# Both directions of a recurrence level in one operation, a pair's gates evacuated raw, and another order of the first block's projections

## The reference

```
f = lb + (1 - lb) * sigmoid(z);  logf = log(max(f, F_TINY));  k = (1 - lb) * sigmoid(-z)
o[t] = sum over s <= t of (q[t] * k[s] * exp(b[t] - b[s])) v[s]      # b = cumsum(logf), q = silu(q_rec)
o_r = o_forward + o_backward; o_r *= rsqrt(mean(o_r * o_r) + EPS); rec = o_r * rec_norm_w * silu(g_rec)
```

## Time and profile before

| | us |
|---|---|
| median of 3 runs | 3002.67 (3001.07 to 3006.88) |
| the profiled execution | 2999.89 |
| its span, first to last instruction | 2998.1 |
| PE / DVE / ACT / POOL busy | 2800.7 / 1654.3 / 1118.8 / 612.9 |
| layer 0 of the first block, first projection matmul to the first of `w_out` | 66.3 to 399.5 |
| layer 1 of the same | 849.8 to 1167.2 |
| last projection matmul of the two | 324.2, 1088.5 |

### The profile page before, as it was taken

How to read it: one execution, slowest core, us unless ns; L and a number is a source line. 1 busy time by engine, 2 the same in 40 slices (tenths; PEclk the granted TensorE clock), 3 DMA queues, 4 the chain that set the end, 5 groups by cost and what they waited for, 6 DMA issues and landing times.

```text
span 2998.1 us, 36465 instructions
## 1 busy us (share of the span) xinstructions
PE 2800.7 (93%) x14716; PEld 2157.6 (72%) x14716; DVE 1654.3 (55%) x3003; ACT 1118.8 (37%) x1875; POOL 612.9 (20%) x338
## 2 busy tenths in 40 slices
PE   3999889999999988999998999989998999999998
PEld 2966667778877766788886878656676878766676
DVE  6767945654464785665456467634425237734424
ACT  3254344322234344443223552243313462343312
POOL 0000024776700000455540231000110131000110
PEclk7999799999999979999999999989999999999999
DMA  7442123544521211344433332111222212121222
GB/s 229 146 125 60 52 85 112 169 140 155 176 83 55 64 55 57 109 140 144 140 127 102 114 113 92 59 61 43 78 77 91 82 43 71 57 85 43 72 72 82
DMA packets 301463, 289.24 MB, mean 96 GB/s; under 512 B 7152, under 2 KB 298096, under 8 KB 301296
## 3 DMA queue, kind: packets, MB, share of 16 engines
q1 hardware_dynamic: 299008, 278.84, 29.2%
q0 software_dynamic: 960, 5.51, 0.5%
q10 hardware_dynamic: 1328, 2.57, 0.3%
HBM read 284.80 MB, written 2.10 MB: 96 GB/s over the span
## 4 chain that ended last, share of the span: by engine, by line
PE 83%; DVE 9%; ACT 4%; POOL 2%; DMA 2%; issue 1%; DVEq 0%; ACTq 0%; POOLq 0%
PE ps L503 81%; PE ps L672 2%; DVE ca L1244 1%; DVE wl L1238 1%; DVE adaacc L1244 1%; DVE recat L1452 1%; POOL raw L1698 1%; DVE hl L1244 1%; POOL raw L1701 1%; ACT wh L836 1%; DMA raw<-in_w_up 1%; DMA xT<-in_xT 0%; ACT rr L836 0%; DVE rawt L1244 0%; DVE s L1491 0%
## 5 line engine op out<-in xcount | busy, mean ns | idle before, releaser
L503 PE MATMUL ps<-hh,wh 128*128 128x512 f32 x2288 | 940.9, 411 | 50.6 <-DVE hl L1244 23.0
L503 PE MATMUL ps<-hh,wl 128*128 128x512 f32 x2288 | 902.4, 394 | 0.0
L503 PE MATMUL ps<-hl,wh 128*128 128x512 f32 x2288 | 902.0, 394 | 0.0
L1238 DVE TENSOR_TENSOR wl<-raw,wh 128x2048 fp32r<-128x2048 f32 (+2 forms) x186 | 443.2, 2383 | 372.3 <-ACT wh L836 371.9
L503 PEld LDWEIGHTS ps<-hh,wh 128*128 128x128 f32 x2288 | 434.9, 190 | 194.0 <-issue 67.9
L503 PEld LDWEIGHTS ps<-hh,wl 128*128 128x128 f32 x2288 | 434.8, 190 | 96.4
L503 PEld LDWEIGHTS ps<-hl,wh 128*128 128x128 f32 x2288 | 436.2, 191 | 89.4 <-issue 7.0
L836 ACT ACTIVATE wh<-raw 128x2048 fp32r<-128x2048 f32 (+2 forms) x186 | 342.6, 1842 | 236.1 <-PE ps L503 142.7
L1698 POOL TENSOR_TENSOR raw<-raw,cond 128x2048 f32<-128x2048 f32 x40 | 186.6, 4664 | 272.5 <-DMA raw<-in_w_ada 272.5
L836 ACT ACTIVATE rawt<-ps 128x512 f32<-128x512 f32 (+1 forms) x106 | 63.3, 597 | 350.4 <-PE ps L503 350.3
L1701 POOL TENSOR_TENSOR raw<-raw 128x1024 f32<-128x1024 f32 x80 | 167.9, 2099 | 6.3
(11 more groups left out here) (229 smaller groups left out, 3772.7 us busy)
## 6 DMA issues: line engine op xcount, KB each, us to landing
raw<-in_w_in SPq DMA_DIRECT2D x74, 1024.0 KB, 5.3
raw<-in_w_ada SPq DMA_DIRECT2D x64, 1024.0 KB, 5.3
raw<-in_w_up SPq DMA_DIRECT2D x44, 1024.0 KB, 5.3
raw<-in_w_in SPq DMA_DIRECT2D x44, 512.0 KB, 5.2
raw<-in_w_out SPq DMA_DIRECT2D x16, 1024.0 KB, 5.2
raw<-in_w_down SPq DMA_DIRECT2D x16, 1024.0 KB, 5.4
stage<-in_w_ada SPq DMA_DIRECT2D x8, 1024.0 KB, 12.3
raw<-in_w_down SPq DMA_DIRECT2D x8, 768.0 KB, 4.6
```

Source lines behind the costliest of these rows:

```text
L503: return e.matmul(o, a, b, start=start, stop=stop, skip_group_check=True)
L1238: return e.tensor_tensor(o, a, b, op)
```

## The change

- Levels: one `rl` unit does both directions. PE makes the same matmuls, into one pair of banks for both directions, even levels into banks 4 and 5 and odd ones into 2 and 3. DVE's queries, keys, totals and conditional copies span both directions in one operation each (`both`).
- The query after silu is kept once, in `M.sg[:, p, :]`; the diagonal's matmuls read it there for both directions, and DVE makes both directions of `recq` in one product, beside the diagonal instead of after it.
- `z` is evacuated raw into `recf`; a new unit `zs` (`gates`) takes both sigmoids later. So the z tiles of pair p wait for level 0 of pair p - 1 instead of level 8. The output and norm of pair p - 1 (`ra`, `ro`, `rn`) are woven around the diagonal of pair p; the square lies in `M.tots[0]`.
- Projections come in the order of `BLOCK1`; `g` tiles are held by `rn` 0, `rn` 1 and `rd` 2.
- `weave` takes, of the side lists that are due, the one with most remaining work; a list whose next unit is an attention score or exponent counts double. `COST` has new figures. This rule holds for the second block too.

The core of the diff (longer removed runs are left out, as they stand above):

```diff
-    "z": (("ACT", 1.25, True),), "q": (("ACT", 0.6, True), ("DVE", 0.7, True), ("ACT", 1.2, True), ("DVE", 2.8, True)),
+    "z": (("ACT", 0.6, True),), "q": (("ACT", 0.6, True), ("DVE", 0.7, True)), "zs": (("ACT", 2.2, True), ("DVE", 2.5, True)),
+    "ra": (("ACT", 2.4, True),),
-    "a": (("ACT", 0.6, True), ("DVE", 0.9, True)), "rd": (("PE", 1.8, True), ("ACT", 1.2, False), ("DVE", 1.4, True)),
-    "rl": (("PE", 1.0, True), ("DVE", 2.1, True)), "ro": (("PE", 2.0, True), ("ACT", 0.6, True)),
+    "a": (("ACT", 0.6, True), ("DVE", 0.9, True)), "rd": (("DVE", 1.2, True), ("PE", 1.8, True), ("ACT", 1.2, False)),
+    "rl": (("PE", 1.6, True), ("DVE", 1.4, True), ("DVE", 1.6, False)), "ro": (("PE", 2.0, True), ("ACT", 0.6, True)),
     "rn": (("PE", 0.9, True), ("ACT", 1.3, True), ("DVE", 1.5, True)), "cv": (("DVE", 3.1, True),),
...
+WEIGHT = {"s1": 2.0, "sx": 2.0}
...
-            first = min(open_, default=None)
+            due = [(sum(left[i]) * WEIGHT.get(sides[i][0][0][0], 1.0), when, i) for when, i in open_ if when <= self.clock["PE"] + 0.2]
+            first = max(due)[1:] if due else None
             main = parts or mains and all(x in done for x in mains[0][3] or ())
-            if first is not None and (first[0] <= self.clock["PE"] + 0.2 or not main):
-                when, i = first
+            if first is not None or not main:
+                when, i = first or min(open_)
                 unit = sides[i].pop(0)[0]
+                left[i].pop(0)
                 done[unit] = ready[i] = self.run(unit, when)
...
+def both(a, first, apart, dims):
+    return bass.AP(a.tensor, a.offset + first, [list(a.ap[0]), [apart, 2]] + dims)
...
     def rec_diagonal(l, p):
-        go.wait_ge(*at("q_in", l, p))
-        go.wait_ge(*at("gates", l, p))
+        go.wait_ge(*at("q_silu", l, p))
+        go.wait_ge(*at("keys", l, p))
         banks_ = [rec_bank(2 + h, ("rd", l, p, h)) for h in range(2)]
         for i in range(NT):
             for d in range(2):
                 for h in range(2):
                     r, sl = rows_of(h), slice(512 * d + 128 * i, 512 * d + 128 * i + 128)
-                    m = mm(banks_[h][:, 128 * i:128 * i + 128], M.reck[r, sl], M.recq[r, sl], d == 0, d == 1)
+                    m = mm(banks_[h][:, 128 * i:128 * i + 128], M.reck[r, sl], M.sg[r, p, 128 * i:128 * i + 128], d == 0, d == 1)
         m.then_inc(*up("pe_rec", ("rd", l, p)))
-    def rec_level(l, p, lv, d):
+    def rec_level(l, p, lv):
         n = 1 << lv
...
+        go.wait_ge(*at("rec_up", l, p, lv - 1))
+        if lv < 8:
+            banks_ = [rec_bank(2 - 2 * (lv % 2) + h, ("rl", l, p, lv, h)) for h in range(2)]
+        for d in range(2):
+            if lv == 8:
+                banks_ = [rec_bank(2 - 2 * d + h, ("rl", l, p, lv, h, d)) for h in range(2)]
+            for x, (i, c0) in enumerate(across(n, d) if lv >= 7 else [(i, 0) for i in range(NT)]):
                 c = 512 * d + 128 * i
...
+                for h in range(2):
+                    r = rows_of(h)
+                    if lv < 7:
+                        m = mm(half(banks_[h][:, 128 * i:128 * i + 128], n, 1 - d), M.reck[r, c:c + 128],
+                               half(M.recq[r, c:c + 128], n, 1 - d), True, True)
+                    else:
+                        o = x * n + (256 * d if lv == 7 else 0)
+                        m = mm(banks_[h][:, o:o + n], M.reck[r, c:c + 128], M.recq[r, 512 * d + c0:512 * d + c0 + n], True, True)
+        m.then_inc(*up("pe_rec", ("rl", l, p, lv)))
...
         if p and o == 0:
...
+            go.wait_ge(*at("rec_total", l, p - 1, 1))
         go.wait_ge(*at("main", ("z", l, p, o)))
-        act(M.recf[:, sl], b[:, :], ACT.Sigmoid)
-        act(M.reck[:, sl], b[:, :], ACT.Sigmoid, scale=-1.0).then_inc(*up("act_z", ("out", ("z", l, p, o)), ("z_in", l, p)))
+        act(M.recf[:, 512 * o:512 * o + 512], bank("z", l, p, o)[:, :], ACT.Copy).then_inc(
+            *up("act_z", ("out", ("z", l, p, o)), ("z_raw", l, p)))
+    def gates(l, p):
+        for event in rec_done(l, p - 1) if p else ():
+            go.wait_ge(*at(*event))
+        go.wait_ge(*at("z_raw", l, p))
+        act(M.reck[:, :], M.recf[:, :], ACT.Sigmoid, scale=-1.0).then_inc(*up("act_z", ("z_keys", l, p)))
+        act(M.recf[:, :], M.recf[:, :], ACT.Sigmoid).then_inc(*up("act_z", ("z_in", l, p)))
     def q(l, p, j):
         go.wait_ge(*at("main", ("q", l, p)))
-        t = tmp_slot(("q", l, p), ("q_in", l, p))
+        t = tmp_slot(("q", l, p), ("q_silu", l, p))
         act(t, bank("q", l, p)[:, :], ACT.Sigmoid).then_inc(*up("act_q", ("q_sig", l, p)))
...
+    def rec_across(l, p, lv=8):
+        go.wait_ge(*at("rl", l, p, lv))
+        for h in range(2):
+            A = M.AT[:, h, 0, :]
+            if lv == 7:
+                act(both(A, 128, 384, [[1280, 2], [1, 128]]), bank("rl", l, p, lv, h)[:, :].rearrange(
+                    "p (d x t) -> p d x t", d=2, x=2), ACT.Copy).then_inc(
+                    *up("act_rec", ("out", ("rl", l, p, lv, h)), ("across", l, p)))
+            for d in range(2) if lv == 8 else ():
+                act(both(A, 1024 * d + 256 * (1 - d), 512, [[1, 256]]), bank("rl", l, p, lv, h, d)[:, :].rearrange(
+                    "p (x t) -> p x t", x=2), ACT.Copy).then_inc(
+                    *up("act_rec", ("out", ("rl", l, p, lv, h, d)), ("across", l, p)))
...
+        tt(M.sg[:, p, :], b[:, :], t, ALU.mult).then_inc(*up("dve_q", ("out", ("q", l, p)), ("q_silu", l, p)))
+    def gates(l, p):
+        go.wait_ge(*at("small", "lb"))
+        go.wait_ge(*at("z_keys", l, p))
+        heads = [(slice(512 * o, 512 * o + 512), 6 * l + 3 * o + p) for o in range(2)]
+        for sl, hd in heads:
+            ts(M.reck[:, sl], M.reck[:, sl], M.lbt[:, 12 + hd:13 + hd], None, ALU.mult).then_inc(*up("dve_z", ("keys", l, p)))
         go.wait_ge(*at("z_in", l, p))
...
+        for sl, hd in heads:
+            ts(M.recf[:, sl], M.recf[:, sl], M.lbt[:, 12 + hd:13 + hd], M.lbt[:, hd:hd + 1], ALU.mult, ALU.add).then_inc(*up("dve_z"))
+        go.wait_ge(*last("dve_z"))
+        ts(M.recf[:, :], M.recf[:, :], 1e-30, None, ALU.max).then_inc(*up("dve_z", ("gates", l, p)))
...
+        if p:
+            go.wait_ge(*at("rl", l, p - 1, 8))
+        go.wait_ge(*at("q_silu", l, p))
+        go.wait_ge(*at("gates", l, p))
+        q = M.sg[:, p:p + 1, :].broadcast_to([128, 2, 512])
+        tt(M.recq[:, :].rearrange("p (d t) -> p d t", d=2), q, M.recf[:, :].rearrange("p (d t) -> p d t", d=2), ALU.mult).then_inc(
+            *up("dve_rec", ("rec_up", l, p, -1), ("rec_total", l, p, 0)))
+    def totals(lv):
+        return (M.recf if lv == 0 else M.tots[(lv - 1) % 2])[:, 0:1024 >> lv]
+    def rec_level(l, p, lv):
+        n, m = 1 << lv, 256 >> lv
         if lv == 8:
             return
...
+        go.wait_ge(*at("rl", l, p, lv))
+        go.wait_ge(*at("rec_total", l, p, lv))
+        T, blocks, once = totals(lv), [[2 * n, m], [1, n]], [[2, m], [0, n]]
+        q = both(M.recq[:, :], n, 512 - n, blocks)
+        tt(q, q, both(T, 0, 2 * m + 1, once), ALU.mult)
+        k = both(M.reck[:, :], 0, 512 + n, blocks)
+        tt(k, k, both(T, 1, 2 * m - 1, once), ALU.mult).then_inc(*up("dve_rec", ("rec_up", l, p, lv)))
+        if lv == 0 and (l or p):
+            go.wait_ge(*at("rec_normed", *((l, p - 1) if p else (l - 1, 2))))
         if lv < 7:
...
+            halves = T.rearrange("p (b w) -> p b w", w=2)
+            tt(totals(lv + 1), halves[:, :, 0], halves[:, :, 1], ALU.mult).then_inc(*up("dve_rec", ("rec_total", l, p, lv + 1)))
+            mk = M.msk[:, 128 * lv:128 * lv + 128].rearrange("p (i t) -> p i t", i=1).broadcast_to([128, NT, 128])
             for h in range(2):
...
+                go.wait_ge(*(at("placed", l, p, lv - 1, h) if lv else at("diagonal", l, p, h)))
+                e.copy_predicated(diagonal(M, h), mk, bank("rl", l, p, lv, h)[:, :].rearrange("p (i t) -> p i t", i=NT)).then_inc(
+                    *up("dve_placed", ("out", ("rl", l, p, lv, h)), ("placed", l, p, lv, h)))
...
+BLOCK1 = (("pair", 0), ("a", 0), ("a", 1), ("iv", 0), ("iv", 1), ("iv", 2), ("qk", 0), ("qk", 1), ("pair", 1), ("pair", 2),
+          ("qk", 2), ("g", 0), ("g", 1), ("g", 2))
...
-        before = [("rl", l, p - 1, 8, d) for d in range(2)] if p else None
+        before = [("rl", l, p - 1, 0)] if p else None
...
+        mains.append(([("g", l, c)], 4, ("g", l, 128 * (c // 2 * 2)) if c != 1 else None, [("rn", l, c) if c < 2 else ("rd", l, 2)]))
...
-        rec.append((("rd", l, p), [("q", l, p), ("z", l, p, 1)]))
+        last = [("rl", l, p - 1, 8)] if p else []
+        rec.append((("zs", l, p), last + [("z", l, p, 1)]))
+        if p:
+            rec.append((("ra", l, p - 1), last))
+            rec.append((("ro", l, p - 1), [("ra", l, p - 1), ("iv", l, 0, 3)]))
+        rec.append((("rd", l, p), [("zs", l, p), ("q", l, p)] + ([("ro", l, p - 1)] if p else [])))
+        if p:
```

(29 more changed lines are left out.)

108 lines of the change are left out of this document (19 added, 89 removed).

## The result

The changed kernel takes 2967.64 us (median of 4 runs, 2965.53 to 2968.83) against 3001.87 for the kernel before beside it: ratio 0.9883, 95% interval 0.9865 to 0.99. It is faster by 34 us, where 52 were forecast.

A forecast was written before the change was run, and what follows sets the result against it. It took TensorE to be the bound, with surplus idleness and lower clock mostly in layer ends, where VectorE works off convolution and recurrence. Gains of 29 and 23 us sum to 52: 3002.7 to 2951 us, forecast range 2930 to 2970.

The forecast's parts named there:

- Merging: Recurrence levels: both directions in one VectorE operation save 13 us of VectorE work in layer 0, bounds 5 and 18.
- The end stretch: End of each first-block layer, from pair 2's diagonal: 64 us with surplus 15, against surpluses of 42 and 39 before.
- without it I estimate 10.3: From the output matmuls' end to the next stage's first matmul: 10.3 us without the layer norm, 16.7 today.
- rival B: End stretch is attention's: the last four tiles set the layer's end, 13 us a layer more, 2977 us; chance 15%.
- the two end stretches shrink to 55 to 70 us: Sign of being right: first-block layers' end stretches, 75.3 and 78.7 us before, shrink to 55 to 70 us.
- Ahead of it, layer 0: Before layer 0's end stretch: surplus 27, less 5 for merging, plus 3 for holding pair 2 until pair 1's level 0.
- Order: First block: convolution inputs right after pair 0, so taps start within 60 us of the layer's start and finish before its end.
- Rival A: Full stretch: a level's VectorE answer stands behind four taps and holds TensorE; costs 79 us, giving 3030 us; chance 10%.
- Rival C: First block: nearly all surplus goes, end surplus 5 and the earlier 27 and 17 halved; 90 us, 2913 us; chance 17%.
- Rival D: Second block loses: top-k rounds issued later delay attention that gate tiles wait for; 10 us a layer, 2971 us; chance 10%.
- I expect 0: Second block, reordered by the planner's new rule: no change, bounds plus or minus 10 us a layer.
- The clock: End stretches, granted 0.68 and 0.74 before: all nine levels at 1.2 GHz would add 8 us a layer, 2967 us.

The follow-up runs named there:

- e2: The changed kernel with the first block's projections back in the old order: 3007 us, all of the gain gone and 5 us besides.
- e4: The changed kernel with the gates' projections of pair p+1 waiting for level 8 of pair p again, instead of level 0: 3010 us, slower by 42 us.
- e3: The changed kernel with each VectorE operation at a recurrence level done for one direction and then the other again: slower by 11.6 us.
- e9: The changed kernel with the planner told that TensorE's diagonal does not wait for VectorE's query product: the time is the same.
- e12: The changed kernel with the second and third value tiles and qk 0 ahead of the convolution inputs, so attention starts earlier: 19 us slower.
- e5: The changed kernel with the third query and key tile between pair 1 and pair 2 instead of behind pair 2: 23 us slower.
- e6: The changed kernel with pair 1 ahead of the third value tile and of qk 0 and 1, and qk 2 behind pair 2: 19 us slower.
- e11: The changed kernel with pairs 0 and 1's square and norm in their gate tile, and only VectorE's rescaling moved behind the next pair's level 0: 5.6 us slower.
- e7: The changed kernel with pairs 0 and 1's square and norm in their gate tile, and the norm unit written behind level 0 in the planner's list: 27 us slower.

## Why the prediction was right in sign, with a gain 18 us too high

What was right: the kernel got faster, and by the parts that the prediction leaned on. Without the order (e2) or the early release (e4) nothing of the gain is left. But 2967.64 lies only 2.4 us inside the range that ended at 2970, and it is there by luck. The two layers gave 24.9 of the 52 us (9.3 of 29, 15.6 of 23). The other 6.2 came from the planner's rule outside of them, for which the sum had 0; without them the time would be some 2974. The terms in turn:

- **Merging:** forecast 13 us of DVE a layer, bounds 5 and 18; measured 14 (after against e3), of which the copies, for which 8 were taken, gave 7.9. From before to after the layers' DVE work fell by 12.0 and 10.7. A copy of 512 columns takes 0.67 us of busy time (56.3 over 84), as the sign said. The Trainium skill's fixed cost of about 150 cycles an instruction (VectorE: DVE Perf Modes, section on the TRN2 errata) gave an estimate of 18; 0.127 us an operation lies below it, above all through the products at 0.065.
- **The end stretch:** the forecast's 64 us begin at pair 2's diagonal, ahead of the last projection. From there after takes 68.7 us in layer 0 and 80.2 in layer 1. Rows of after that bound the pieces, layer 0 and then layer 1:

```profile
322.01 2.06 PE L516 MATMUL ps<-recg,reck 64*128 64x128 f32 x32
...
325.91 2.00 PE L516 MATMUL ps<-recq,reck 64*128 64x64 f32 x32
...
364.40 2.00 PE L516 MATMUL ps<-recq,reck 64*128 64x256 f32 x16
...
369.36 3.65 PE L516 MATMUL ps<-recat,recv 128*64 128x512 f32 x16 [2.10 <-ACT recat L852]
```

```profile
1061.43 2.06 PE L516 MATMUL ps<-recg,reck 64*128 64x128 f32 x32
...
1066.13 2.00 PE L516 MATMUL ps<-recq,reck 64*128 64x64 f32 x32 [0.73 <-ACT recat L852]
...
1108.92 2.06 PE L516 MATMUL ps<-recq,reck 64*128 64x256 f32 x16
...
1114.61 3.65 PE L516 MATMUL ps<-recat,recv 128*64 128x512 f32 x16 [1.38 <-ACT recat L852]
```

```
us                                   forecast  layer 0  layer 1
diagonal to level 0                    3.2       3.9      4.7
level 0 to level 8, eight steps       47.0      38.5     42.8
level 8 to the output matmuls          3.5       5.0      5.7
output matmuls                         0         3.65     3.65
behind them, to w_out                 10.3      17.7     23.3
together                              64.0      68.7     80.2
```

- The near total of layer 0 hides misses that offset one another. The eight steps had 26 us of chain, 13 of foreign units and 8 of lower clock; all nine levels of layer 0 ran at the full clock, and of layer 1's two did not (3.68 us for 2.00, and 2.08 for 1.16). The steps were 4.8 us on average in layer 0, inside 3.3 to 5, but 3.4 to 7.2 one by one. The 3.65 us of the output's own matmuls are missing from the forecast's 43, and its last level, taken at 1.1 us, measured 2.0.
- The mis-sized term is "without it I estimate 10.3" behind the output matmuls: 17.7 and 23.3 us, at a granted clock of 0.81 and 0.71. It is the largest excess in either layer; the surplus from the diagonal on is 17 and 25 us, where 15 were taken for each. That is rival B in small. In the trace of after three attention tiles follow there one after the other, the first of layer 1 standing 4.27 us:

```profile
1120.31 1.09 PE L516 MATMUL ps<-att_p,va 128*64 128x128 f32 x16
...
1125.68 1.85 PE L688 MATMUL ps<-cst_r,att_s 128*128 128x128 f32 x8 [4.27 <-DVE att_s L1266]
1128.30 2.08 PE L516 MATMUL ps<-ka,qa 64*128 64x512 f32 x4 [0.78 <-ACT att_p L852]
1131.28 1.98 PE L516 MATMUL ps<-att_p,va 128*64 128x128 f32 x16 [0.90 <-DVE stt L1522]
```

- The sign "the two end stretches shrink to 55 to 70 us" failed. From the last projection, where the prediction had put their start, they are 42.8 and 52.2, shorter than that; from the diagonal 68.7 and 80.2, the second longer.
- **Ahead of it, layer 0:** forecast 27 - 5 + 3 = 25, measured 43.8, the largest miss. The 3 us for the hold were 17 (227 to 267 us), as the norm, priced at "nothing new", and the lower clock came with it; and the query product beside the diagonal got a queue ahead of it that the sum had not (5.49 us and a level at the lower clock; e9 takes both away). In layer 1, without modulation sums, 17 - 2 + 3 = 18 measured 19.0.
- **The step behind both:** the sum treated the stretches as if each could be won alone. The runs show one stock of work under which waits are hidden. e9 won 13 us at one place and lost 10 at another, e12 won 12 and 20 in the tails and lost 26 and 23 in the rest of the same layers, e5 and e6 likewise. In none of the thirteen changed kernels was layer 0's surplus below 57.8 or layer 1's below 40.6; the forecast had 40 and 33. What sets that floor, the chains or only this planner's way to write them, stays open.
- **Order:** the first tap came at 141.9 us, 75 into the layer, not within 60, since nearly all of pair 0's levels, and not a few, lay ahead of it; the taps were still out of the end, and that carried the gain (e2).
- **Rival A** did not come at its price of 79 us, but its sign did, once: the 5.49 us at 96.3 are a wait for the query product with projections behind it, though for modulation sums and a split, not for taps. It is the only wait on `recq` or `reck` above 1 us ahead of the last projection of layer 0; in layer 1 there is one too, of 1.33. The taps lie where projections cover them; e2 shows what they do where nothing does.
- **Rival C** did not come: the surplus left is 61 and 44 us, more than the forecast's 40 and 33. Its own sum was 3 us short as well, since 27 and 17 halved, against the forecast's 25 and 18, are worth 21 and not 18.
- **Rival D** did not come. The rule won 6 to 9 us outside the layers, within the bounds given, but "I expect 0" had no room for it.
- **The clock** in the end stretches was 0.92 and 0.77, and e11 prices it at 4.6 us for one tail. The Trainium skill (TensorE: Matmul & The Clock Gate, Part 1) has the clock fall after idleness; the trace agrees, with 0.71 in the 20 us of the hold, in which PE idles 8, and 1.00 from 267 to 307 us. e11 shows that two kernels of the same order on PE with the same waits can differ in it.

## What to carry to other kernels

Before adding up what several stalls would give, ask what work covers each of them, and whether it is the same work: here none of the stalls that were removed alone (e5, e7, e9, e11) made the kernel faster, and changes that were worth 16 and -5 us alone gave 34 together. When a planner writes the order, a wrong dependence in its costs (a product taken to stand ahead of a matmul) shows up as a wait of several microseconds, but its repair must be judged by the whole layer. Take serial work out of the stretch that has no cover, but leave enough of the parallel work for its end.

## What the runs showed of the hardware

Making one in-place product of 512 columns out of two of 256 saves 0.065 us, one conditional copy out of two 0.187: the operations differ in what merging is worth. By their durations the products would save more: 0.419 us for 256 columns (e3) and 0.690 for 512 (after), so 0.148 for two made one. Back to back the starts are only 0.33 and 0.60 us apart, as each starts before the one ahead of it has ended. The granted clock is a cost of its own at the end of a layer: 0.84 or 0.64 over the same 110 matmuls, 21.3 or 25.9 us.
